# A norm moved behind its matrix product: gained residual halves for the second feed-forward and the last gate

## What is computed

```python
x = x + mixed @ w_out[i]
h2 = rms_norm_2(x, g_mlp[i])
x = x + jnp.square(jax.nn.relu(h2 @ w_ff1[i])) @ w_ff2[i]
gate_p = jax.nn.sigmoid(rms_norm_2(x, g_ple[i]) @ w_ple_gate[i])
x = x + gate_p * (p[i] @ w_ple[i])
return rms_norm_2(x, g_final)
```

## Time and profile before

| | us |
|---|---|
| median of 3 runs (955.3 to 955.63) | 955.35 |
| the profiled execution, its own time | 955.68 |
| its span in the trace | 954.4 |
| PE busy, of the span | 930.7 |
| DVE busy | 646.0 |
| ACT busy | 478.7 |
| POOL busy | 73.2 |

### The profile page before, as it was taken

How to read it: one execution, slowest core, us unless ns; L and a number is a source line. 1 busy time by engine, 2 the same in 40 slices (tenths; PEclk the granted TensorE clock), 3 DMA queues, 4 the chain that set the end, 5 groups by cost and what they waited for, 6 DMA issues and landing times.

```text
span 954.4 us, 17982 instructions
## 1 busy us (share of the span) xinstructions
PE 930.7 (98%) x7334; PEld 889.2 (93%) x7334; DVE 646.0 (68%) x1096; ACT 478.7 (50%) x865; POOL 73.2 (8%) x133
## 2 busy tenths in 40 slices
PE   8999999998999999999999999999999999999996
PEld 6899988997999999997999979999999999999996
DVE  6654575657877777768588866575657656556567
ACT  5355445544655545454466743554346444444454
POOL 4122000223000000001000100000102000000002
PEclk9999999999999999999999999999999999999999
DMA  7543443443465555552644453455544655655531
GB/s 273 186 147 111 136 138 121 145 147 134 145 211 178 191 184 188 178 188 62 203 133 134 138 179 102 164 191 178 190 152 155 221 180 189 187 187 186 178 110 66
DMA packets 43985, 154.73 MB, mean 162 GB/s; under 512 B 4736, under 2 KB 7296, under 8 KB 43776
## 3 DMA queue, kind: packets, MB, share of 16 engines
q1 hardware_dynamic: 43904, 153.59, 49.3%
HBM read 152.52 MB, written 1.05 MB: 161 GB/s over the span
## 4 chain that ended last, share of the span: by engine, by line
PE 89%; DVE 4%; ACT 3%; DMA 1%; issue 1%; POOL 1%; SPq 0%; DVEq 0%; ACTq 0%
PE bank L219 89%; DMA raw<-in_wts 1%; DVE wl L1209 1%; POOL tmpb L1745 1%; ACT wh L766 1%; DVE tmpb L1428 1%; DVE hT L1431 0%; ACT rb L772 0%; DVE hT L1703 0%; ACT rb L774 0%; DVE tmpb L1226 0%; DVE tmpb L1395 0%; ACT xnh L782 0%; DVE tmpb L1396 0%; ACT xnh L907 0%
## 5 line engine op out<-in xcount | busy, mean ns | idle before, releaser
L1209 DVE TENSOR_TENSOR wl<-raw,wh 128x1024 fp32r<-128x1024 f32 x285 | 352.5, 1239 | 166.0 <-ACT wh L766 164.2
L219 PE MATMUL bank<-xnh,wh 128*128 128x256 f32 (+2 forms) x1448 | 410.9, 285 | 2.9 <-ACT xnh L782 1.1
L219 PE MATMUL bank<-xnh,wl 128*128 128x256 f32 (+2 forms) x1448 | 405.5, 282 | 0.0
L219 PE MATMUL bank<-xnl,wh 128*128 128x256 f32 (+2 forms) x1448 | 399.0, 282 | 0.0
L766 ACT ACTIVATE wh<-raw 128x1024 fp32r<-128x1024 f32 x250 | 262.8, 1053 | 157.4 <-PE bank L219 154.8
L219 PEld LDWEIGHTS bank<-xnh,wh 128*128 128x128 f32 x1448 | 273.1, 189 | 7.9 <-issue 4.5
L219 PEld LDWEIGHTS bank<-xnh,wl 128*128 128x128 f32 x1448 | 273.8, 189 | 0.0
L219 PEld LDWEIGHTS bank<-xnl,wh 128*128 128x128 f32 x1448 | 269.4, 189 | 0.3
L219 PE MATMUL bank<-a2h,wl 128*128 128x256 f32 x496 | 139.8, 282 | 0.0
L219 PE MATMUL bank<-a2h,wh 128*128 128x256 f32 x496 | 139.7, 282 | 0.0
L219 PE MATMUL bank<-a2l,wh 128*128 128x256 f32 x496 | 139.5, 281 | 0.0
(11 more groups left out here) (206 smaller groups left out, 975.8 us busy)
## 6 DMA issues: line engine op xcount, KB each, us to landing
raw<-in_wts SPq DMA_DIRECT2D x285, 512.0 KB, 3.6
csb<-in_cst SPq DMA_DIRECT2D x1, 1428.0 KB, 10.8
hT<-in_xT SPq DMA_DIRECT2D x2, 544.0 KB, 4.5
out<-hT SPq DMA_DIRECT2D x3, 256.0 KB, 2.1
qk<-in_pT SPq DMA_DIRECT2D x1, 256.0 KB, 3.7
out<-hT SPq DMA_DIRECT2D x2, 128.0 KB, 1.8
gr<-in_lamv SPq DMA_DIRECT2D x1, 128.0 KB, 10.6
ccol<-in_fcst SPq DMA_DIRECT2D x1, 126.0 KB, 4.8
```

The source lines that it names most:

```text
L219: return e.matmul(o, lhsT, rhs, start=start, stop=stop, skip_group_check=True)
L1209: e.tensor_tensor(lo, src, hi.bitcast(F32), ALU.subtract).then_inc(s_lo, 1)
```

## The change

The factor of a norm that belongs to a token is the same for all features, so it may be applied after the product. The halves are now made of residual times gain, without the root: ACT `gained_hi` (L1134 of the new file: Identity with a column of gains as its scale), DVE `gained_lo` (L1663: residual times gain minus the high half). They are made tile by tile as the residual tiles come, inside the loops that add and square. For instance 5 they go to `a1h`/`a1l`, for instance 6 to `xnh`/`xnl`; the halves of p move to `a2h`/`a2l`, places 4 and 5. Both `warm`s and `normalise` for the two instances are gone. The root comes in later: in the feed-forward DVE computes max(PSUM, 0) * root (L1686) and ACT squares it; in the last gate DVE multiplies PSUM by the root (L1712, new semaphore `s_gq`), then ACT takes the Sigmoid from SBUF. PE takes the last ones of instance 5 after the four `ple`, and the ones of instance 6 one by one behind each k of the `group`.

```diff
+            def group(i0, outs, n0, n1, inst, xh=None, xl=None, after=None):
+                xh, xl = xh or XH(n0, n1), xl or XL(n0, n1)
...
+                    if after:
+                        after(k)
...
-            e.wait_ge(s_sqa, 36 + 8)
-            mm(bank[7][:, 0:S], ones, qk[:, 3 + 7 % 4, 0:S], False, True).then_inc(s_sum, 1)
-
             def ple(i, m, b):
-                t = tile(i, bank[b][:, 0:S], A1[0], A1[1], [2 * (m % 4), 2 * (m % 4) + 1], kx=[0, 1])
+                t = tile(i, bank[b][:, 0:S], A2[0], A2[1], [2 * (m % 4), 2 * (m % 4) + 1], kx=[4, 5])
                 t.then_inc(s_blk if m % 4 == 3 else s_pt, 1)
 
             e.wait_ge(s_pl, 2)
             for m in range(4):
                 e.wait_ge(s_x2, m + 2)
                 ple(B_PLE0, m, 1 + m)
+            e.wait_ge(s_sqa, 36 + 8)
+            mm(bank[7][:, 0:S], ones, qk[:, 3 + 7 % 4, 0:S], False, True).then_inc(s_sum, 1)
 
 
             e.wait_ge(s_x2, 8)
-            warm(8, 0)
             e.wait_ge(s_pp, 1)
-            group(B_FF2, [bank[b][:, 0:S] for b in range(2)], 0, S, 5)
+            group(B_FF2, [bank[b][:, 0:S] for b in range(2)], 0, S, 5, A1[0], A1[1])
             for j in range(FF2 + LAG2):
                 if 1 < j < FF2:
                     if j < 4:
                         e.wait_ge(s_pp, j)
                     else:
                         e.wait_ge(s_rl, j - 3)
-                    tile(up2(j), bank[j % 4][:, 0:S], XH(0, S), XL(0, S), range(KT)).then_inc(s_blk, 1)
+                    tile(up2(j), bank[j % 4][:, 0:S], A1[0], A1[1], range(KT)).then_inc(s_blk, 1)
...
-            e.wait_ge(s_x3, 2)
-            for m in range(KT):
-                e.wait_ge(s_sqa, 44 + m + 1)
-                t = mm(bank[4][:, 0:S], ones, qk[:, m, 0:S], m == 0, m == KT - 1)
-            t.then_inc(s_sum, 1)
-
-
-            GB = [0, 1, 2, 3, 5, 6, 7]
-            e.wait_ge(s_pp, 5)
-            warm(8, 0)
+
+
+            def gate_sum(k):
+                if k == 0:
+                    e.wait_ge(s_x3, 2)
+                e.wait_ge(s_sqa, 44 + k + 1)
+                t = mm(bank[4][:, 0:S], ones, qk[:, k, 0:S], k == 0, k == KT - 1)
+                if k == KT - 1:
+                    t.then_inc(s_sum, 1)
+
             e.wait_ge(s_pp, 6)
-            group(B_GP, [bank[b][:, 0:S] for b in range(2)], 0, S, 6)
+            group(B_GP, [bank[b][:, 0:S] for b in range(2)], 0, S, 6, after=gate_sum)
...
-                    e.wait_ge(s_gg, 1)
+                    e.wait_ge(s_gq, 1)
                 tile(B_GP + m, bank[GB[m % 7]][:, 0:S], XH(0, S), XL(0, S), range(KT)).then_inc(s_blk, 1)
                 if m == 7:
                     e.wait_ge(s_sqp, 10 + 5)
+                    e.wait_ge(s_rs, 7)
                     mm(bank[4][:, 0:S], ones, qk[:, 0, 0:S], True, False)
...
+                e.activation(a2h[:, 4 + k, :], qk[:, k, 0:S], ACT.Copy).then_inc(s_ph, 1)
+
+            def gained_hi(k, dst, gcol):
+                e.activation(dst, xk(k), ACT.Identity, scale=ccol[:, gcol + k:gcol + k + 1]).then_inc(s_xhi, 1)
+
+            for m in range(9):
+                if 3 <= m < 8:
                     hi_to(B_WOUT2 + m + 4)
                 if m:
                     e.wait_ge(s_x2, m)
+                    gained_hi(m - 1, a1h[:, m - 1, 0:S], COL_GMLP)
                     if m - 1 >= 5:
                         e.wait_ge(s_sqp, 5 + m - 5)
                     e.activation(qk[:, 2 if m == 1 else 3 + (m - 1) % 4, 0:S], xk(m - 1), ACT.Square).then_inc(s_sqa, 1)
...
             root(5, bank[7][:, 0:S], S, 1024)
-            halves_hi(5, S)
 
             hi_to(B_FF2 + 5)
             for j in range(FF2 + LAG2):
                 if j < FF2:
                     if j > 1:
                         hi_to(up2(j) + 4)
-                    e.wait_ge(s_blk, up2(j) + 1)
-                    if j >= 6:
-                        e.wait_ge(s_zl, FF1 + j - 5)
-                    e.activation(tmpb[:, j % 6, 0:S], bank[j % 4][:, 0:S], ACT.Relu).then_inc(s_rl, 1)
+                    x = tmpb[:, j % 6, 0:S]
+                    e.wait_ge(s_rl, j + 1)
+                    e.activation(x, x, ACT.Square).then_inc(s_zq, 1)
                 if 0 < j <= FF2:
...
             for m in range(8):
                 e.wait_ge(s_x3, m + 1)
+                gained_hi(m, xnh[:, m, 0:S], COL_GPLE)
                 e.activation(qk[:, m, 0:S], xk(m), ACT.Square).then_inc(s_sqa, 1)
-            hi_to(B_PLE1 + 4)
+                if m == 5:
+                    hi_to(B_PLE1 + 4)
             for m in range(4, 8):
                 ple_copy(m, m - 4)
             root(6, bank[4][:, 0:S], S, 1024)
-            halves_hi(6, S)
             hi_to(B_GP + 4)
             e.preload_act_table_set(SIG_SET)
             hi_to(B_GP + 5)
-            GB = [0, 1, 2, 3, 5, 6, 7]
             for m in range(8):
                 if m >= 2:
                     hi_to(B_GP + m + 4)
-                e.wait_ge(s_blk, B_GP + m + 1)
-                if m >= 6:
-                    e.wait_ge(s_xf, m - 5)
-                e.activation(tmpb[:, m % 6, 0:S], bank[GB[m % 7]][:, 0:S], ACT.Sigmoid).then_inc(s_gg, 1)
+                x = tmpb[:, m % 6, 0:S]
+                e.wait_ge(s_gq, m + 1)
+                e.activation(x, x, ACT.Sigmoid).then_inc(s_gg, 1)
                 if m:
...
+            def gained_lo(inst, k, hi, lo, gcol):
+                e.wait_ge(s_xhi, 8 * inst + k + 1)
+                e.scalar_tensor_tensor(lo, xk(k), ccol[:, gcol + k:gcol + k + 1], hi.bitcast(F32), ALU.mult,
+                                       ALU.subtract).then_inc(s_xlo, 1)
+
+            for m in range(9):
+                if m < 8:
+                    if m >= 3:
+                        lo_to(B_WOUT2 + m + 4)
+                    e.wait_ge(s_blk, B_WOUT2 + m + 1)
+                    e.tensor_tensor(xk(m), xk(m), bank[W_OUT_BANK(m)][:, 0:S], ALU.add).then_inc(s_x2, 1)
+                if m:
+                    gained_lo(5, m - 1, a1h[:, m - 1, 0:S], a1l[:, m - 1, 0:S], COL_GMLP)
...
-                    x = tmpb[:, j % 6, 0:S]
-                    e.wait_ge(s_rl, j + 1)
-                    e.tensor_tensor(x, x, x, ALU.mult).then_inc(s_zq, 1)
+                    e.wait_ge(s_blk, up2(j) + 1)
+                    if j == 0:
+                        e.wait_ge(s_rs, 6)
+                    if j >= 6:
+                        e.wait_ge(s_zl, FF1 + j - 5)
+                    e.scalar_tensor_tensor(tmpb[:, j % 6, 0:S], bank[j % 4][:, 0:S], 0.0, rb[:, 1, 0:S], ALU.max,
+                                           ALU.mult).then_inc(s_rl, 1)
...
+            for m in range(9):
+                if m < 8:
+                    if m < 6:
+                        e.wait_ge(s_down, 3 + m // 2 + 1)
+                    else:
+                        e.wait_ge(s_blk, B_PLE1)
+                    e.tensor_tensor(xk(m), xk(m), FD(m), ALU.add).then_inc(s_x3, 1)
+                if m:
+                    gained_lo(6, m - 1, xnh[:, m - 1, 0:S], xnl[:, m - 1, 0:S], COL_GPLE)
             lo_to(B_GP + 5)
             for m in range(8):
                 if m >= 2:
                     lo_to(B_GP + m + 4)
                 x = tmpb[:, m % 6, 0:S]
+                e.wait_ge(s_blk, B_GP + m + 1)
+                if m == 0:
+                    e.wait_ge(s_rs, 7)
+                if m >= 6:
+                    e.wait_ge(s_xf, m - 5)
+                e.tensor_tensor(x, bank[GB[m % 7]][:, 0:S], rb[:, 0, 0:S], ALU.mult).then_inc(s_gq, 1)
                 e.wait_ge(s_gg, m + 1)
                 e.wait_ge(s_pp, 8)
                 e.tensor_tensor(x, x, pp(m), ALU.mult).then_inc(s_gm, 1)
```

More of the change, by code:

```diff
@@ L214, in program @@
         W_OUT_BANK = lambda m: m % 7
+        GB = (0, 1, 2, 3, 5, 6, 7)
         def tensor_engine(e):
@@ L236, in tile @@
                 return t
-            def group(i0, outs, n0, n1, inst):
+            XH = lambda n0, n1: (lambda k: xnh[:, k, n0:n1])
+            XL = lambda n0, n1: (lambda k: xnl[:, k, n0:n1])
+            def group(i0, outs, n0, n1, inst, xh=None, xl=None, after=None):
+                xh, xl = xh or XH(n0, n1), xl or XL(n0, n1)
                 for k in range(KT):
@@ L1127, in scalar_engine @@
             for k in range(2):
-                e.activation(a1h[:, k, 0:S], qk[:, k, 0:S], ACT.Copy).then_inc(s_ph, 1)
-            for m in range(8):
-                if m >= 3:
+                e.activation(a2h[:, 4 + k, :], qk[:, k, 0:S], ACT.Copy).then_inc(s_ph, 1)
[3 more added lines that the diff above has]
+                if 3 <= m < 8:
                     hi_to(B_WOUT2 + m + 4)
@@ L1136, in scalar_engine @@
                     e.activation(qk[:, 2 if m == 1 else 3 + (m - 1) % 4, 0:S], xk(m - 1), ACT.Square).then_inc(s_sqa, 1)
-            e.wait_ge(s_x2, 8)
-            e.wait_ge(s_sqp, 5 + 3)
-            e.activation(qk[:, 3 + 7 % 4, 0:S], xk(7), ACT.Square).then_inc(s_sqa, 1)
             def ple_copy(m, b):
@@ L1656, in vector_engine @@
                 e.wait_ge(s_ph, k + 1)
```

(12 more changed lines are left out.)

18 lines of the change are left out of this document (4 added, 14 removed).

## The result

The change makes the kernel one per cent slower: 965.05 us in the median of 4 runs (964.58 to 966.71) beside 955.45 us for the kernel before (4 runs, 955.3 to 955.63). The ratio is 1.0103, with a 95% interval of 1.0086 to 1.0121. The forecast was 963.0 in a range of 959.0 to 966.5. The profiled execution took 965.46, its span is 964.1 (before: 954.4), 9.7 us more.

A forecast was written before the change was run, and what follows sets the result against it. PE was taken to bound the kernel, with DVE and ACT exposed behind the last tile. The terms -2.0 + 2.3 + 5.8 + 1.5 sum to +7.6, giving 963.0 us in the median, range 959.0 to 966.5.

The forecast's parts named there:

- the central case: Whole kernel: 963.0 us in the median, own range 960.5 to 965.5, chance 0.55.
- the falling clock: Rival: PE's wait before the last group drops the clock to half; +9 to +11 us, 965.5, chance 0.2.
- C: Last group's end to last addition: root and blocks come behind the group, DVE and ACT round trips set the pace; +5.8.
- D: Loop at the end: POOL's additions slow DVE operations beside them, three costing 0.5 each; +1.5, bounds 0 and 2.75.
- A: To the up-projection: group starts at 729.8 instead of 731.78, block 208 wait 0.8 longer; -2.0, bounds -2.9 to -1.2.
- B: To the last group's end: starts 1.8 sooner, but ones inside make it 9.8 us; +2.3, bounds +1.0 to +3.5.
- the forecast's own signs of being wrong: Feed-forward span changes, PE's six last tiles run without a gap, or clock below 1 for over a third of last group.
- 0, and the same 173 us: Second feed-forward: the engines' swapped PSUM and SBUF reads are covered by free time, so its span stays 173 us.
- The rival's lesser price: Last group at half clock for a third of its 9.8 us: put at +1.7, against +9.8 for all of it.
- The rule cited in D: DVE operations with two SBUF inputs and GpSimd exclude each other at a shared port pair; products reading PSUM can't be stopped.
- From the last addition to the end nothing changes: End of the kernel, behind the last addition: no change in time.
- The rival of a hidden loop: End loop: DVE and ACT overlap more, PE keeps the pace; only +1 to +4 us, 958, chance 0.15.

The follow-up runs named there:

- ff_only: Only the second feed-forward as changed, the last gate as in the kernel before: 954.27 us beside 955.77, ratio 0.9982.
- warm_gap: The changed kernel with 14 useless matmuls in PE's wait ahead of the last group: 963.15 us, ratio 1.0075.
- gate_only: Only the last gate as changed, the second feed-forward as in the kernel before: 967.17 us, ratio 1.0117.
- pool_off: The changed kernel where POOL adds the squares of the last norm in only 8 of 256 columns: 963.61 us, ratio 1.0078.
- after: The kernel with the whole change, against the kernel before: 965.05 us in the median, ratio 1.0103.
- lo_between: The changed kernel, DVE making the next low half behind the product with the root, ACT its high half sooner: 962.79 us, ratio 1.0074.
- ones_ahead: The changed kernel with the last gate's eight ones ahead of the group, in PE's wait: 957.03 us beside 955.53, ratio 1.0013.
- warm_two: warm_gap plus 12 useless matmuls behind PE's last gate tile: 962.58 us, ratio 1.0074.
- both: The changed kernel with ones_ahead and lo_between together: 952.79 us beside 955.53, ratio 0.9973.

## Why the prediction was right, and where not

The verdict (slower, 0.90) and the range held. What came true is not the central case but the one the forecast had as a rival with 0.2, the falling clock. Of the sum, +7.6, the parts C and D were right and A was right by two errors, which is luck; B and the end were short, and this makes the 2.1 us between 963.0 and 965.05. Two of the forecast's own signs of being wrong came up: the span of the feed-forward changed, and in the profiled execution the granted clock was below 1 for 5.7 of the group's 11.65 us, more than a third.

*A, predicted -2.0.* To the group it gained more: the start moved from 731.78 to 729.21, 2.6 us, of which 0.2 are the head start of the execution, so 2.35 instead of 2.0. The wait at block 208 is 0.77 longer (1.00 instead of 0.23), where 0.8 was said. A gained half takes 0.49 to 0.51, 0.40 to 0.42 from its start to the next, and a pair with its square 0.71 to 0.73, as assumed. The surplus is the switching between ones and split matmuls, put at 0.1 each time, which costs nothing (below). "0, and the same 173 us" for the feed-forward failed: it takes 0.6 more, and by the prediction's own condition that is an error. The two leave -1.9, without the head start -1.7. That this part alone is a gain is shown by ff_only, -1.5 in the median.

*B, predicted +2.3, measured +3.85.* The start was right: PE waits for the copies behind the pairs on ACT, idle for 3.52 us where 3.8 was said. Two sizes in the group were off. Switching to ones and back, put at 0.1 each, costs nothing: the next split matmul starts 0.25 behind one of ones and the one after it 0.30 later, together 0.55, which is 0.43 and 0.118. So the group is 9.0 us instead of 9.8 (warm_gap). And the clock fell: +2.6 in the profiled execution, +1.6 in gate_only and pool_off. The rival's lesser price, +1.7, was nearer than the full +9.8, since the clock comes back while the group runs; but it does not follow from its own words, for a third of 9.8 us at double length is +3.3. With -0.2 and -0.8 and +2.6 the +2.3 becomes 3.9; that the switches were overpriced by 0.8 hid part of the clock's cost, again by luck. (With 0.2 for each of seven switches the upper bound of B would also be +3.0, not +3.5.) The reason given against this rival, that the wait is hardly longer than 3.5 us, did not hold. In each of the four profiles in which this wait was left in place the clock fell, in two of them (after and lo_between) 2.4 and 2.5 us behind the last matmul, with PE still idle. The Trainium skill ("TensorE: Matmul & The Clock Gate", Part 1) has half rate as the default state that activity lifts. The trace agrees: the clock came back at 924.2, 5.7 us after the group had begun at half rate.

*C and D, predicted +5.8 and +1.5, measured +7.2 together.* The first product with the root stands 5.8 behind the group (5.7). Steps of 1.70 and 3.30 to 3.34 stand where 1.69 and 3.35 were said, three of the additions count with 0.48 (0.5), and PE's waits for low halves are 1.50, 0.26 and 0.24 ahead of blocks 282 to 284, besides 0.48 ahead of 280. pool_off shows D; ones_ahead and lo_between show the two parts of C: 3.4 us go with the root ahead of the group's end, and PE's waits for blocks 282 to 284 with the order in the loop. The rule cited in D is borne out at the output projection: beside POOL's addition an addition that reads PSUM took 0.41 as usual, and a low half with two inputs from SBUF 0.63 instead of 0.48. The products with the root are no test of it, since none of them ran while POOL was adding.

*"From the last addition to the end nothing changes"* failed by 0.55. PE has nothing to do for 3.1 us behind its last tile, the clock falls a second time at 954.9, the last ones run at half pace, and the root starts 2.19 behind the last addition instead of 1.67 (957.70 and 955.51; before 948.03 and 946.36); warm_two shows it. The prediction had seen the longer loop and PE's last tile ahead of it, and did not ask what PE does meanwhile.

The rival of a hidden loop (0.15) fell with the order of the operations, as argued. It nearly becomes true when that order and the place of the ones are changed: in both PE runs its last six tiles without a wait, and from the group's end to the last addition it is 19.0 us instead of 18.15 before the change and 25.36 with it.

## To carry to other kernels

A scaling factor moved behind a product takes the norm off the way to the first matmul and puts it on the way of the first result. Check what stands between the last matmul and that result on each in-order queue, and leave the reduction ahead of the group if its engine would otherwise wait there: it costs nothing in the wait, keeps the clock up, and frees the root. In a round trip between two engines, put work that is due anyway into the partner's part of the trip. Before a useless matmul is removed, read how long the wait is without it.

## What the runs showed of the hardware

- The same wait of 3.52 or 3.53 us ahead of the last group let the granted clock fall to half in four profiles of four, but not at the same point. In after and lo_between it fell 2.4 and 2.5 us behind PE's last matmul, during the wait (at 917.4 and 918.3); in gate_only and pool_off it fell 3.7 and 4.8 us behind it, when the group had begun (at 920.8 and 919.9). It was full again at 924.2, 925.2, 924.2 and 923.3. So the group paid 1.6 to 2.7 us for the same wait. 14 matmuls of 128 columns in 3.29 us, or 8 of ones on the squares in 3.84, kept it full.
- A DVE addition or product with two inputs from SBUF took 0.89 to 0.97 instead of 0.42 where one of POOL's additions ran at its start; an addition with one input from PSUM kept its 0.41. POOL's addition took 0.72 to 0.74 there, and up to 1.21 in the kernel before, where it started during one of DVE's low halves. A new order of DVE's work did not avoid the collisions; it moved two of them from slack onto products that count.
- A full fp32 matmul of 256 columns and a split one can follow each other without a price: 0.43 us from one of ones to the next, 0.25 from one of ones to a split one and 0.30 from that to the next, which is 0.43 and 0.118 together.
- The pace of matmuls changed by 0.3% when only the places of buffers in SBUF were changed, at full clock and without a wait (179.84 and 180.32 us for the same matmuls, and 193.5 and 194.05 in the first feed-forward). The Trainium skill ("SBUF — State Buffer", Who interferes with whom) says that PE waits for no one at its ports; what makes this difference no run here shows.
- Executions whose code is the same so far differ by up to 1.6 us after 250 us (250.61 in after, 252.21 in ones_ahead), which is why kernels half a microsecond apart could not be told from each other by their medians.
